# Joints in front of the up-projections of a hybrid decoder: centring and token sums on GpSimd, pieces interleaved by K tile, three product runs alternated

## The reference

```python
for i in range(DEPTH):                      # 2 layers
    mix = delta_mixer(x, ...) if i % 2 == 0 else shortconv_mixer(x, ...)
    x = layer_norm(ALPHA * x + mix, ln_mix_g[i], ln_mix_b[i])
    f = conv_ffn(x, ...)                    # x @ w_up (1024 -> 5632), conv, silu gate, @ w_down
    x = layer_norm(ALPHA * x + f, ln_ffn_g[i], ln_ffn_b[i])
    x = x + (p[i] @ ple_w_proj[i]) * sigmoid(x @ ple_w_gate[i])

def layer_norm(x, g, b):
    mu = mean(x); var = mean(square(x - mu))
    return (x - mu) * rsqrt(var + LN_EPS) * g + b
```

## Time and profile before

| | |
|---|---|
| median of 3 executions | 1735.3 us (1732.84 to 1736.59) |
| profiled execution, its own time | 1735.66 us |
| its span, first to last instruction | 1733.6 us |
| mean granted TensorE clock | 0.995 |
| TensorE busy | 1692.2 us, 98% |
| VectorE busy | 1075.4 us, 62% |
| ScalarE busy | 460.7 us, 27% |
| GpSimd busy | 241.5 us, 14% |

### The profile page before, as it was taken

The page is one execution under the profiler, slowest core; times in us unless marked ns, Lnnn a source line. Parts: engine busy times, 40 slices in busy tenths (PEclk is TensorE's granted clock), DMA queues, the critical chain, the costliest instruction groups (busy, mean ns, idle before and its releaser), DMA issues. The chain is left out here.

```text
span 1733.6 us, 22781 instructions
## 1 busy us (share of the span) xinstructions
PE 1692.2 (98%) x8243; PEld 1321.8 (76%) x8243; DVE 1075.4 (62%) x2062; ACT 460.7 (27%) x1084; POOL 241.5 (14%) x537
## 2 busy tenths in 40 slices
PE   8999999999899999999999999999999999999999
PEld 5777678877677777777777777776777777777777
DVE  4866775676876766662336655468766667633375
ACT  2433406742422222210033111114222222200051
POOL 0111216652110000001100000012100000001100
PEclk9999999989999999999999999999999999999999
DMA  4232210331222222242140322211222222321211
GB/s 155 74 115 87 82 61 14 111 124 37 72 73 79 79 86 73 74 144 83 50 135 1 115 80 83 75 49 50 73 73 74 85 78 81 139 96 67 86 49 55
DMA packets 45645, 139.40 MB, mean 80 GB/s; under 512 B 4944, under 2 KB 12240, under 8 KB 45536
## 3 DMA queue, kind: packets, MB, share of 16 engines
q1 hardware_dynamic: 42864, 133.36, 23.6%
q10 hardware_dynamic: 2672, 4.61, 0.8%
HBM read 129.63 MB, written 8.31 MB: 80 GB/s over the span
## 5 line engine op out<-in xcount | busy, mean ns | idle before, releaser
L274 PE MATMUL bank<-z,ring 128*128 128x288 f32 x1952 | 509.5, 408 | 10.2 <-DVE z L392 2.8
L274 PEld LDWEIGHTS bank<-z,ring 128*128 128x128 f32 x1952 | 370.9, 191 | 117.8 <-issue 8.0
L274 PE MATMUL bank<-x,ring 128*128 128x288 f32 x1632 | 428.0, 409 | 11.4 <-DMA x<-in_x 4.9
L274 PEld LDWEIGHTS bank<-x,ring 128*128 128x128 f32 x1632 | 310.3, 191 | 102.0 <-issue 6.6
L2191 DVE SCALAR_TENSOR_TENSOR scratch<-scratch 128x592 f32<-128x592 f32 x176 | 146.2, 832 | 25.6 <-ACT scratch L2135 24.0
L274 PE MATMUL bank<-y,ring 128*128 128x288 f32 x616 | 156.4, 406 | 0.0
L274 PE MATMUL bank<-big,ring 128*128 128x288 f32 x536 | 137.8, 412 | 4.5 <-PEq L1774 2.3
L274 PEld LDWEIGHTS bank<-y,ring 128*128 128x128 f32 x616 | 117.0, 190 | 32.3
L274 PEld LDWEIGHTS bank<-big,ring 128*128 128x128 f32 x536 | 102.9, 193 | 35.4 <-issue 5.0
L2135 ACT ACTIVATE scratch<-scratch 128x592 f32<-128x592 f32 x88 | 69.4, 789 | 90.7 <-DVE scratch L2165 89.1
L2225 POOL COPY scratch<-scratch 128x2 f32<-128x2 f32 x88 | 26.0, 296 | 465.8 <-ACT scratch L2121 465.8
(11 more groups left out here) (372 smaller groups left out, 2172.4 us busy)
## 6 DMA issues: line engine op xcount, KB each, us to landing
ring<-in_w_up SPq DMA_DIRECT2D x88, 512.0 KB, 3.6
ring<-in_w_scin SPq DMA_DIRECT2D x24, 512.0 KB, 3.6
ring<-in_w_qkv SPq DMA_DIRECT2D x21, 512.0 KB, 3.6
ring<-in_w_down SPq DMA_DIRECT2D x12, 704.0 KB, 4.1
scratch<-in_w_down SPq DMA_DIRECT2D x12, 704.0 KB, 5.4
ring<-in_w_z SPq DMA_DIRECT2D x8, 512.0 KB, 3.6
big<-in_st_S SPq DMA_DIRECT2D x16, 256.0 KB, 6.0
out_dn_S_sample<-big SPq DMA_DIRECT2D x16, 256.0 KB, 3.0
```

Of the source, the lines that this page charges most:

```text
L274: last = pe.matmul(bank[:, 0:HALF], w[:, k * P:(k + 1) * P], rhs(k), start=start and k == 0, stop=k == self.depth - 1, skip_group_check=no ...
```

## The change

It applies to the two norms in front of the up-projections (even `number`), with one exception named below.

- GpSimd centres six pieces of half 1 (positions 2 to 7) in place of two; VectorE keeps two. The order of the pieces in half 1 becomes 0, 4, 1, 5, 2, 6, 3, 7.
- GpSimd makes the four `token1` sums, and `sum1` and `sum2` of step 1; `sum3` of step 1 moves behind `sum4(0)` on VectorE.
- `centre_pool` waits for the mean, and no longer for VectorE's two centrings. This holds for all four norms.
- `second_half_up_dve` is VectorE's order for the scalings and token sums; the `token4` sums move in front of the reads of p6.
- TensorE alternates p6(0), p6(1) and p5(0) K tile by K tile (`p6_both_p5`), and p5(1) moves from behind p7(1) to in front of p4(0).

```diff
--- before.py
+++ after.py
@@ -325,19 +325,25 @@
                 if ks is None or self.depth - 1 in ks:
                     last.then_inc(product6, 1)
 
-            def p6_both(self, pe):
+            def p6_both_p5(self, pe):
 
 
                 for i in range(2):
                     pe.wait_ge(sum2_made, self.base + i + 1)
                     if self.base + i >= 2:
                         pe.wait_ge(c21_read, self.base + i - 1)
+                pe.wait_ge(sum1_made, self.base + 1)
+                if self.base >= 2:
+                    pe.wait_ge(c12_read, self.base - 1)
                 for k in range(self.depth):
                     pe.wait_ge(token2_made, self.token_base + k + 1)
                     for i in range(2):
                         last = self.run(pe, BANK[2 + (self.base + i) % 2], i, "s2", self.t(2), True, None, (k,))
                         if k == self.depth - 1:
                             last.then_inc(product6, 1)
+                    pe.wait_ge(token1_made, self.token_base + k + 1)
+                    last = self.run(pe, BANK[4 + self.base % 2], 0, "s1", self.t(1), True, None, (k,))
+                last.then_inc(product5, 1)
 
             def p7(self, pe, i):
                 g = self.base + i
@@ -1983,11 +1989,14 @@
         class LayerNorm:
 
 
-            POOL_PIECES = ((), (2, 3))
-            ORDER = (tuple(range(DT)), tuple(range(DT)))
-
             def __init__(self, number, which, residual):
                 self.number, self.which, self.residual = number, which, residual
+                before_up = number % 2 == 0
+                late = tuple(m for k in range(KH) for m in (k, KH + k)) if before_up else tuple(range(DT))
+                self.ORDER = (tuple(range(DT)), late)
+                self.POOL_PIECES = ((), tuple(range(2, DT)) if before_up else (2, 3))
+                self.by_pool = (number + 1) // 2 * (DT - 2) + number // 2 * 2
+                self.by_dve = 2 * DT * number - self.by_pool
 
             def nth(self, half, m):
                 return 16 * self.number + DT * half + self.ORDER[half].index(m) + 1
@@ -2067,7 +2076,7 @@
             def centre_pool(self, pool):
 
 
-                pool.wait_ge(ln_centred_dve, 14 * self.number + DT + 2)
+                pool.wait_ge(ln_mean, 4 * self.number + 4)
                 for n in self.POOL_PIECES[1]:
                     y = self.residual.piece(self.ORDER[1][n], 1)
                     pool.tensor_tensor(y, y, mu[:, HALF:TOK], ALU.subtract).then_inc(ln_centred, 1)
@@ -2078,10 +2087,10 @@
                 for n in range(DT)[some]:
                     m = self.ORDER[half][n]
                     if n in self.POOL_PIECES[half]:
-                        dve.wait_ge(ln_centred, 2 * self.number + self.POOL_PIECES[half].index(n) + 1)
+                        dve.wait_ge(ln_centred, self.by_pool + self.POOL_PIECES[half].index(n) + 1)
                     else:
                         own = [x for x in range(DT) if x not in self.POOL_PIECES[half]]
-                        dve.wait_ge(ln_centred_dve, 14 * self.number + DT * half + own.index(n) + 1)
+                        dve.wait_ge(ln_centred_dve, self.by_dve + DT * half + own.index(n) + 1)
                     y = self.residual.piece(m, half)
                     dve.tensor_tensor(y, y, rs[:, cols], ALU.mult).then_inc(ln_scaled, 1)
 
@@ -2557,14 +2566,17 @@
             d.p2(pe, 0, ready_high)
             d.p2(pe, 1)
             if sums:
-                d.p5(pe, 0)
-                d.p6_both(pe)
+                d.p6_both_p5(pe)
                 d.p7(pe, 0)
-            else:
-                d.p6(pe, 0)
-                d.p6(pe, 1)
-                d.p7(pe, 0)
-                d.p5(pe, 0)
+                d.p5(pe, 1)
+                d.p4(pe, 0)
+                d.p3(pe, 0)
+                d.p7(pe, 1)
+                return
+            d.p6(pe, 0)
+            d.p6(pe, 1)
+            d.p7(pe, 0)
+            d.p5(pe, 0)
             d.p4(pe, 0)
             d.p3(pe, 0)
             d.p7(pe, 1)
@@ -2787,13 +2799,14 @@
 
         def up_dve(dve, layer):
             f, d = ffn[layer], up[layer]
-            second_half_dve(dve, norm[2 * layer], d, True)
+            second_half_up_dve(dve, norm[2 * layer], d)
             f.u1(dve, 0)
             f.u1(dve, 1)
             d.sum4(dve, 0)
+            dve.wait_ge(sum1_made, d.base + 2)
+            dve.wait_ge(sum2_made, d.base + 2)
+            d.sum3(dve, 1)
             f.u2(dve, 0)
-            for k in range(KH):
-                d.token4(dve, k)
             f.c22(dve, 0)
             d.sum4(dve, 1)
             f.c21(dve, 0)
@@ -2967,21 +2980,30 @@
             r.add_square(dve, 14)
             next_dense.sum2(dve, 0)
             next_dense.sum3(dve, 0)
-            next_dense.sum1(dve, 1)
-            next_dense.sum2(dve, 1)
-            next_dense.sum3(dve, 1)
-
-        def second_half_dve(dve, n, d, fifth_first):
+
+        def second_half_up_dve(dve, n, d):
 
 
             n.variance(dve, 1)
             n.centre_dve(dve, 1, slice(0, 2))
             n.inverse(dve, 1)
             n.scale(dve, 1, slice(0, 4))
-            if fifth_first:
-                for k in range(KH):
-                    dve.wait_ge(ln_ready, n.nth(1, k))
-                    d.token1(dve, k)
+            for k in range(KH):
+                dve.wait_ge(ln_ready, n.nth(1, KH + k))
+                d.token3(dve, k)
+                d.token2(dve, k)
+                if k < 2:
+                    n.scale(dve, 1, slice(2 * k + 4, 2 * k + 6))
+            for k in range(KH):
+                d.token4(dve, k)
+
+        def second_half_dve(dve, n, d):
+
+
+            n.variance(dve, 1)
+            n.centre_dve(dve, 1, slice(0, 2))
+            n.inverse(dve, 1)
+            n.scale(dve, 1, slice(0, 4))
             for k in range(KH + 1):
                 if k < KH:
                     n.centre_dve(dve, 1, slice(KH + k, KH + k + 1))
@@ -3006,7 +3028,7 @@
             d, g = ple[layer], gate[layer]
             d.sums123(dve, 0)
             d.sums123(dve, 1)
-            second_half_dve(dve, norm[2 * layer + 1], d, False)
+            second_half_dve(dve, norm[2 * layer + 1], d)
             for k in range(KH):
                 d.token4(dve, k)
             d.sum4(dve, 0)
@@ -3132,18 +3154,20 @@
             end_residual_dve(dve, residual[2], up[1])
 
 
-        def mixer_pool(pool, r):
-            n = norm[r.number]
-            for x in range(10):
+        def mixer_pool(pool, r, d):
+            for x in range(15):
                 r.add_piece(pool, x)
-            r.add_piece(pool, 10)
-            r.add_piece(pool, 11)
-            for x in range(12, 15):
-                r.add_piece(pool, x)
+            pool.wait_ge(sum1_made, d.base + 1)
+            d.sum1(pool, 1)
+            pool.wait_ge(sum2_made, d.base + 1)
+            d.sum2(pool, 1)
 
         def up_pool(pool, layer):
-            f = ffn[layer]
-            norm[2 * layer].centre_pool(pool)
+            f, n = ffn[layer], norm[2 * layer]
+            n.centre_pool(pool)
+            for k in range(KH):
+                pool.wait_ge(ln_ready, n.nth(1, k))
+                up[layer].token1(pool, k)
             for s in range(2):
                 for x in range(2):
                     pool.memset(EXT[s][x][:, SAMPLE_COLS:PROMPT_AT], 0.0).then_inc(pads, 1)
@@ -3325,12 +3349,12 @@
 
             @block.gpsimd
             def _(pool):
-                mixer_pool(pool, residual[0])
+                mixer_pool(pool, residual[0], up[0])
                 up_pool(pool, 0)
                 down_pool(pool, 0)
                 norm[1].centre_pool(pool)
                 shortconv_pool(pool)
-                mixer_pool(pool, residual[2])
+                mixer_pool(pool, residual[2], up[1])
                 up_pool(pool, 1)
                 down_pool(pool, 1)
                 norm[3].centre_pool(pool)
```

## The result

The changed kernel takes 1741.14 us (median of 8, 1738.06 to 1742.76) against 1735.94 for the kernel before: ratio 1.003, 95% interval 1.002 to 1.0041. It is slower by 5.2 us. The forecast was 1740.9 from a median of 1735.3, 5.6 us slower.

A forecast was written before the change was run, and what follows sets the result against it. TensorE, busy 98% of the span, was taken as the bound, idling on VectorE at two joints. Per joint 0.8 (order) + 0.3 + 1.7 (clock) = 2.8, for two 5.6 us slower: 1740.9 us, range 1733.5 to 1742.8.

The forecast's parts named there:

- The stops: At each joint, every GpSimd 128x288 sum stops a two-operand VectorE operation 0.60 us; p7 at 464.16, before 463.98.
- rival (b): At the joints VectorE and GpSimd hardly meet; p7 starts at 459.3, total 1730.6 us, faster; chance 0.08.
- Rival (d): At the joints VectorE's stops last for all of the GpSimd instruction: 1743.7 us; chance 0.05.
- The load: Behind p3 and p7 of pair 1, p1 of pair 2 waits 2.54 us for weights, 2.1 more than before.
- Rival (c): p1 of pair 2 does not wait for the load, a wait of 0.43 stays: 1734.2 us; chance 0.08.
- The order of work together: From p7's start and the load wait, p1 of pair 2 comes 0.8 us later per joint.
- The clock: Half clock for about 3.4 us behind both long idle times per joint: 0.3 us before p6, 1.7 behind the load wait.
- rival (a) with one fall: As forecast, but the clock stays up at one of the load waits: 1739.2 us; chance 0.15.
- the signs of being right: Load wait about 2.5 us with half clock behind, stretched VectorE operations 444 to 462, reciprocal after 450.1, p7 near 464.2.
- The parts at nothing: Behind down-projections, centre_pool's earlier wait makes VectorE some 0.8 us late, hidden by its 5.15 us idle; counted as nothing.

The follow-up runs named there:

- e2: Changed kernel with seven extra matmuls, results overwritten, in TensorE's long idle time before the first token2 of each joint; ratio to the kernel before 1.0019.
- e3: Changed kernel with token1 sums on VectorE behind the last token2, p6 of both pairs alternated, p5 of pair 0 behind them; ratio to the kernel before 1.0015.
- e4: Changed kernel with the wait of centre_pool put back behind VectorE's two centrings; ratio to the kernel before 1.0044 (5 executions).
- e1: Changed kernel with p5 of pair 1 behind p7 of pair 1 again; ratio to the kernel before 1.001.
- b1: Changed kernel with TensorE's order p7(0), p7(1), p4(0), p3(0), p5(1), p4(1), then p1 of pair 2; ratio to the kernel before 0.9996.
- e5: Changed kernel with extra matmuls in both idle times: seven before the first token2, four behind p7 of pair 1; ratio to the kernel before 1.0011.
- c3: b1 with token1 and pair 1's weight sums on VectorE, p5(0) behind both p7, five extra matmuls in the idle time; ratio to the kernel before 0.9993.
- c1: b1 with token1 on VectorE and p5 of pair 0 only behind both p7, no extra matmuls; 1731.96 against 1735.16 us for the kernel before, ratio 0.998.

## Why the prediction was right

**The stops.** One GpSimd sum stops a two-operand VectorE operation for 0.60 us: measured 1.07 - 0.46 = 0.61. GpSimd's 128x512 sum, set at 1.26, took 1.27. The maximum is stopped too (0.68). Behind the start of the sums over tokens (444.79 before, 443.46 after) the reciprocal was put at 5.67 us and came at 5.88, p6 at 12.11 and came at 12.35. p7 was put at 19.37, against 19.19 before; it came at 19.86 and 20.82, and at 19.73 in e2 with a full clock. So p7 came later than before and not earlier, and rival (b), no meeting of the two engines, is out. Rival (d), stops as long as the whole instruction, would have made token2 1.24 us long; it took 1.07. On "the whole instruction" the Trainium skill (page "SBUF — State Buffer", section "SBUF: two separate sides") and the rows differ: they agree that one engine blocks the other, but the stop, 0.61 us, is shorter than the 0.79 us that the trace gives the GpSimd sum. One reading of the prediction is off: three scalings of 2.24 us in place of 1.2 beside two GpSimd sums are 0.52 us for each, not 0.60; the 0.60 comes from VectorE's 128x512 sum at 442.80 (1.28 - 0.69 = 0.59).

**The load.** Put at 2.54 us in the changed kernel; the profiled executions show 1.81, 2.25 (changed), 2.17, 2.41 (e2), 2.34, 2.10 (e3), 2.20, 2.16 (e4). Part of the difference is bookkeeping: 2.54 counts a product as 1.94 us, while its last record in the trace ends 0.16 later, so in the trace's terms 2.38 was forecast. The rest is the load: from the end of p3 to p1 of pair 2 these eight joints take 3.92 to 4.51 us, 4.28 on average, and the 4.48 taken was near the upper edge. Rival (c) is out by the waits themselves, and by e1 and b1, which shrink them.

**The order of work together**, 0.8 us per joint, 1.6 in all: e5, with the clock kept up, shows 1.9 by the ratio and 1.7 by its joints. Of the 0.8, p7's share was put at 0.2 and is 0.5 in e2, and the load's at 0.6 and is 0.4 and 0.6 there.

**The clock.** Here the mechanism held, but two sizes were off, and they made good for each other by luck. In front of p6 I allowed 0 to 0.65 us per joint and took 0.3; the first joint lost 0.13, the second 1.10, because the clock stayed low there for 6.8 us (1210.0 to 1216.9), not 3.4. Of the eight such joints in the profiles of the changed kernel, e1, e4 and b1, two had the long stretch (the other is the second joint of e1). e2 puts the two joints together at 1.9 us in the median. Behind the load wait I took 1.7 us each, 3.4 in all. The price of one fall was right (1.7 us in e2), its frequency was not: filling the waits gave 1.4. The clock fell there in e4 at both joints, in e2 at the first, in e3 at the second, and in the profiled execution of the changed kernel at neither, though half clock behind the load wait stood among the signs of being right. So it falls in some executions and not in others, and the likeliest single case (both) was priced too high as a median. As far as the mean clock tells, the median execution is rival (a) with one fall, which was put at 1739.2; the number came out at the forecast because the other two parts cost more than their price. 1.6 + 0.6 + 3.4 = 5.6 was forecast; 1.9 + 1.9 + 1.4 = 5.2 is what the ratios show, and 1.7 + 1.2 + 1.7 = 4.6 what the profiles show with one fall at two load waits.

**The range.** Rival (c) less half a microsecond is 1733.7, not the 1733.5 of the lower end; nothing hangs on it.

**The parts at nothing.** Behind the down-projection the reciprocal started 912.82 - 910.52 = 2.30 us behind the variance, where it was 1.46 before, 0.84 later for a forecast of 0.8, and TensorE waited for nothing there.

## What to carry to other kernels

Before moving elementwise work to GpSimd, count the two-operand VectorE operations that will run beside it: here each GpSimd sum took 0.6 us from VectorE, against 0.37 us for doing the same small sum itself, so token1 on GpSimd did not pay (e3). The two 128x512 weight sums seem to have paid, by about 1 us per joint in c3, which also moved a third sum. When products are reordered, list what each product's end releases, and count the work left between that release and its user: one product moved in front of p3 made the load wait 1.4 and 1.8 us longer. A long idle time of TensorE can have a second price in the clock: four waits of 0.49 to 1.78 us before the change left it full, the one wait of 3.72 us that took their place did not.

## What the runs showed of the hardware that was not expected

The granted clock stayed at half for 6.8 us at the second joint behind an idle time of 3.73 us, and for 3.4 us at the first behind 3.72, with the same order of work. It fell at all twelve joints with an idle time of 2.5 us or more in front of p6 (3.7 to 3.8 in the changed kernel, e1, e4 and b1, 2.55 in e3 and c1). Behind load waits of 1.8 to 2.4 us it fell in four of eight cases seen in the profiles of the changed kernel, e2, e3 and e4, and not by length: it fell behind 2.10 (e3) and stayed full behind 2.41 (e2). GpSimd's small copies of history ran from 459.86 to 461.04 at the first joint of the changed kernel, and the token2 at 460.51 beside them took 0.47 us against 0.46 undisturbed.
